# One quarter of the tokens' experts by gathered rows on VectorE, three quarters as dense native fp32 and split products

## The chip, the cores and the metric

The program runs on one core of a Trainium2 chip. Its engines are TensorE (PE, with its weight loads as PEld), VectorE (DVE), ScalarE (ACT), GpSimd (POOL) and SyncE (SP, which here only issues DMAs). The metric is device microseconds of one execution, as a median of several. Everything is float32 at input and output.

## The reference, cut to what matters

The reference runs two two-layer blocks on 256 tokens of width 1024. The first block is not touched. Each layer of the second is a mixing sublayer and then this expert layer, and only the expert layer's arithmetic is arranged anew:

```python
def peer_ffn(xn, wq, sub_keys, u_tab, v_tab):        # xn: 256 tokens x 1024
    q = matmul(xt, wq).reshape(t, 8, 2, 128)          # 8 heads, two half queries
    scores = einsum('thcd,hcnd->thcn', q, sub_keys)   # 128 keys for each half
    sv, si = lax.top_k(scores, 16)
    cand_s = sv[:, :, 0, :, None] + sv[:, :, 1, None, :]
    cand_i = si[:, :, 0, :, None] * 128 + si[:, :, 1, None, :]
    best_s, best_p = lax.top_k(cand_s, 16)            # 16 experts of 16384 a head
    idx = take_along_axis(cand_i, best_p, axis=-1)
    gate = softmax(best_s, axis=-1)
    act = einsum('td,thkd->thk', xb, u_tab[ib])       # 8 x 16 = 128 experts a token
    wgt = gelu(act) * gb
    y = einsum('thk,thkd->td', wgt, v_tab[ib])
```

u_tab and v_tab have 16384 rows of 1024 in each layer. An expert's number is i * 128 + j. A tile of u or v below is [128 x 1024] of 4 bytes, 512 KB: the 128 experts that share a j.

## The kernel before

Each expert layer has three stages, and they run one after the other with a barrier between them.

**choose_stage** streams 16 tiles of query weights (HC = 16) and then the first 28 tiles of u (EARLY = 28) through a ring of four slots (RAW = 4). TensorE works in split precision: ScalarE writes each half tile rounded to fp32r (the high part, line 332), another engine subtracts it from the tile (the low part, line 341; in this stage GpSimd does it), and `product` (line 218) issues three fp32r matmuls, high by high, high by low, low by high. Two split tiles are kept (SPLIT = 2). VectorE meanwhile finds the best keys of each head and then runs a long chain of small operations over candidates, places and gates. TensorE turns three results at the end (line 2320) and uses the last u tile after that.

**scatter_stage** builds, for each token, the 128 x 128 matrix of gates as a native fp32 product of two one-hot matrices (line 2529), in lots of four tokens: 64 lots. VectorE makes the one-hots (line 2498), GpSimd multiplies gates in (line 2517), ScalarE copies the result out (line 2546). Two native fp32 matmuls of 384 columns stand at its end (`hold_clock`, line 2532).

**experts_stage** computes every expert for every token, and the gates, most of them zero, pick. It streams 228 tiles: v tiles 0 to 27, whose activations choose_stage has made, and then u and v in turns for the other 100. A u tile (`activate`) is 24 fp32r matmuls of 256 columns (tokens), on operands h2T (the normalised input, split) and the split tile. ScalarE's gelu (line 2648), then VectorE's multiplication by the gates (2693), rounding (2696) and low part (2698) give the weights of that tile in `chunk`. A v tile (`combine`) is 12 fp32r matmuls of 512 columns: two blocks of 128 tokens by two halves of the width by three passes. Four banks of PSUM hold the sums over all v tiles. ScalarE makes the high part of every tile and VectorE the low part, each in two halves, two tiles ahead of TensorE. SyncE refills a slot as soon as its tile's low part is made. GpSimd has nothing to do in this stage. At its end 16 transposes (line 2635) bring the sums back, and VectorE adds them to x2T (2722).

The order of a u/v pair in the loop is v of j-1, u of j+1, v of j, u of j+2: the weights that a v tile needs come from the u tile two matmul groups earlier.

## Time and profile before

| | us |
|---|---|
| median of 3 runs | 3447.21 |
| lowest and highest | 3446.87, 3452.45 |
| the profiled execution, its own time | 3456.25 |
| its span, first to last instruction | 3454.5 |
| choose, scatter and experts stages of layer 1 | about 76 (after the queries), 87, 642 |

The profile is one execution, read as spans of instructions per engine. "Busy" is the time in which an engine had an instruction under way; idle time is put down to what released the engine after it. TensorE's matmuls overlap, so the time of a group of them is read from the first start to the last end in the timeline, and not as a count times the mean of one.

### The profile page before, as it was taken

The numbers are of one execution on the slowest core, as the hardware profiler recorded it, in microseconds if no ns is written. First come the engines' busy times: TensorE is split into PE (matmuls) and PEld (weight loads), VectorE is DVE, ScalarE is ACT, GpSimd is POOL, SyncE is SP. The second block draws the span as 40 slices with busy tenths as digits, with TensorE's granted clock in tenths as the row PEclk, the third lists the DMA queues.
The fourth block names the chain that finished last, engine by engine and source line by source line (L and its number), as shares of the span: only waits on it lengthen the run. The fifth ranks groups of instructions, "written<-read, shape, count | busy, mean of one in ns | idle before, by whom it ended". The sixth has DMA issues, their size and how long they took to land. (4 is left out here: it accounts for less than half of the span.)

```text
span 3454.5 us, 64762 instructions
## 1 busy us (share of the span) xinstructions
PE 3314.5 (96%) x20448; PEld 2879.7 (83%) x20448; DVE 2427.3 (70%) x4837; ACT 1759.6 (51%) x3349; POOL 543.1 (16%) x444
## 2 busy tenths in 40 slices
PE   7999999999999999999899999999999899999999
PEld 6767777778769998889878989988889878989988
DVE  5567777767566775659877677676659877777676
ACT  4453343333356654656754444444656764454454
POOL 0000000000000000658820000000648830000000
PEclk7999999999899998999999999999999999999999
DMA  5125444435115454335135555555335235555554
GB/s 204 44 69 182 159 138 135 147 122 164 55 61 173 159 174 155 122 117 171 54 128 187 185 187 188 184 187 179 123 116 171 67 115 186 185 188 187 185 187 152
DMA packets 139224, 508.83 MB, mean 147 GB/s; under 512 B 15968, under 2 KB 16352, under 8 KB 138208
## 3 DMA queue, kind: packets, MB, share of 16 engines
q1 hardware_dynamic: 138384, 504.56, 45.0%
q10 hardware_dynamic: 720, 2.71, 0.2%
q8 instruction: 71, 1.16, 0.1%
q14 instruction: 49, 0.40, 0.0%
HBM read 506.16 MB, written 1.05 MB: 147 GB/s over the span
## 5 line engine op out<-in xcount | busy, mean ns | idle before, releaser
L332 ACT ACTIVATE split<-ring 128x512 fp32r<-128x512 f32 (+1 forms) x1660 | 1038.3, 629 | 1390.2 <-PE ps L218 1343.5
L341 DVE TENSOR_TENSOR split<-ring,split 128x512 fp32r<-128x512 f32 (+1 forms) x1364 | 932.0, 687 | 642.9 <-ACT split L332 628.2
L218 PEld LDWEIGHTS ps<-h2T,split 128*128 128x128 f32 x7776 | 946.8, 188 | 30.8 <-DVE h2T L579 5.4
L218 PE MATMUL ps<-h2T,split 128*128 128x256 f32 x7776 | 962.0, 281 | 4.7 <-DVE gates L2135 3.1
L218 PE MATMUL ps<-split,chunk 128*128 128x512 f32 x3072 | 750.4, 395 | 0.0
L341 POOL TENSOR_TENSOR split<-ring,split 128x512 fp32r<-128x512 f32 x296 | 389.6, 1334 | 2174.0 <-ACT split L332 2167.8
L218 PEld LDWEIGHTS ps<-split,chunk 128*128 128x128 f32 x3072 | 561.5, 187 | 124.6 <-DVE chunk L2678 1.1
L218 PE MATMUL ps<-hT,split 128*128 128x512 f32 (+1 forms) x3504 | 631.6, 341 | 6.3 <-DVEq L316 3.4
L218 PEld LDWEIGHTS ps<-hT,split 128*128 128x128 f32 x3504 | 545.1, 190 | 92.6 <-DVE hT L581 7.6
L218 PE MATMUL ps<-act_chunk,split 128*128 128x512 f32 (+1 forms) x1056 | 190.8, 342 | 0.0
L218 PEld LDWEIGHTS ps<-act_chunk,split 128*128 128x128 f32 x1056 | 164.8, 191 | 22.3
L2529 PE MATMUL ps<-ring 128*128 128x128 f32 x1024 | 144.6, 290 | 31.4 <-POOL ring L2517 12.3
L2529 PEld LDWEIGHTS ps<-ring 128*128 128x128 f32 x1024 | 127.7, 197 | 48.2 <-DVE ring L2498 42.4
L2517 POOL TENSOR_TENSOR ring<-ring,slot_gate 128x512 f32<-128x512 f32 x128 | 133.0, 1039 | 32.3 <-DVE ring L2498 32.2
L2693 DVE TENSOR_TENSOR gated<-gelu,gates 128x256 f32<-128x256 f32 x200 | 123.3, 617 | 0.0
L2498 DVE TENSOR_TENSOR ring<-ps,slot_i 128x512 f32<-128x512 f32 x128 | 87.5, 684 | 11.8 <-PEq L2521 11.5
L2698 DVE TENSOR_TENSOR chunk<-gated,chunk 128x256 fp32r<-128x256 f32 x200 | 85.1, 425 | 6.8
L2546 ACT ACTIVATE gates<-ps 128x400 f32 (+1 forms) x128 | 64.4, 503 | 25.8 <-PE ps L2529 24.3
L2648 ACT ACTIVATE gelu<-ps 128x256 f32<-128x256 f32 x200 | 72.8, 364 | 0.0
L2498 DVE TENSOR_TENSOR ring<-ps,slot_j 128x384 f32<-128x384 f32 x128 | 69.8, 545 | 0.0
L218 PE MATMUL ps<-branchT,split 128*128 128x512 f32 (+1 forms) x384 | 69.5, 336 | 0.0
L218 PE MATMUL ps<-y_chunk,split 128*128 128x512 f32 (+1 forms) x384 | 69.5, 340 | 0.0
(353 smaller groups left out, 3166.7 us busy)
## 6 DMA issues: line engine op xcount, KB each, us to landing
ring<-peer_uv SPq DMA_DIRECT2D x456, 512.0 KB, 3.5
ring<-w_up SPq DMA_DIRECT2D x88, 512.0 KB, 3.7
ring<-w_choose SPq DMA_DIRECT2D x88, 512.0 KB, 4.1
ring<-w_mixing SPq DMA_DIRECT2D x68, 512.0 KB, 3.6
ring<-w_merge SPq DMA_DIRECT2D x64, 512.0 KB, 4.1
ring<-w_down SPq DMA_DIRECT2D x44, 512.0 KB, 3.7
mix_row_ring<-w_mod SPq DMA_DIRECT2D x40, 512.0 KB, 3.7
ffn_row_ring<-w_mod SPq DMA_DIRECT2D x40, 512.0 KB, 3.9
```

What stands on the lines that cost most here:

```text
L218: ins = nc.tensor.matmul(out, lhsT(a), rhs(b), start=first and n == 0, stop=last and n == len(PASSES) - 1)
L332: self.nc.scalar.activation(self.split[:, self.half_slot(s), 0, cols], self.ring[:, self.slot(s), cols], ACT.Copy).then_inc(self.high_read ...
L341: (ops or self.nc.vector).tensor_tensor(self.split[:, self.half_slot(s), 1, cols], self.ring[:, self.slot(s), cols], self.split[:, self.ha ...
L2498: nc.vector.tensor_tensor(hot[:, n * lot + first:(n + 1) * lot, :], iota[:, 0:many, :], keys, ALU.is_equal).then_inc(one_hot, 1)
L2517: nc.gpsimd.tensor_tensor(hot, hot, gates, ALU.mult).then_inc(gated, 1)
L2529: last = nc.tensor.matmul(k.ps[:, n, u * NK:(u + 1) * NK], k.hot_i[:, n * lot + u, :], k.hot_j[:, n * lot + u, :], start=True, stop=True)
L2546: nc.scalar.activation(k.dense[:, bass.ds(token(i, n) * late, lot * late)].rearrange("p (t j) -> p t j", t=lot), k.ps[:, n, :].rearrange(" ...
L2648: nc.scalar.activation(k.gelu[:, buf, :], k.ps[:, buf, 0:SEQ], ACT.Gelu_apprx_tanh).then_inc(gelu_done, 1)
L2693: nc.vector.tensor_tensor(k.gated[:, :], k.gelu[:, buf, :], dense[:, :, bass.ds(j - EARLY, 1)].rearrange("p t j -> p (t j)"), ALU.mult).th ...
L2698: nc.vector.tensor_tensor(low, k.gated[:, :], high.bitcast(F32), ALU.subtract).then_inc(weighted, 1)
```

## The change

Tokens 0 to 191 (DENSE = 192) stay in the dense scheme. The 128 experts of each of the last 64 tokens are fetched as rows. Partition p of the row buffers stands for token 192 + p mod 64 and for one half of its 128 experts, so that 64 gathers of u rows and 64 of v rows, each 128 rows of 4 KB (512 KB), serve a layer.

- GpSimd issues the 128 gathers of a layer in experts_stage, by indices `row_at` that VectorE makes in choose_stage, into six slots; each waits until the row six before has been used.
- VectorE takes a dot product of each u row with its token (`dot`, 1024 elements, a multiplication with a running sum), and after one gelu and one multiplication by gates adds each v row times its weight (`add_row`). Their places among the 228 tiles are fixed by a table: one at every v tile from 28 on, one in four before, and 22 more; the first 64 are dots and the last 64 are additions (the table has one place more than it needs).
- u tiles, the early ones in choose_stage and the 100 in experts_stage, are 8 native fp32 matmuls of 192 columns on the raw tile and an unsplit copy of the input (h2F). No high or low part is made of them, and their slot is free only when TensorE has used it.
- A v tile is 10 fp32r matmuls of 512 columns: tokens 0 to 127 keep three passes a half; tokens 128 to 191 stand with their high and low parts side by side in one operand of 128, which meets v's high and low part, two passes a half.
- scatter_stage handles 192 tokens, 48 lots. choose_stage spreads the 64 tokens' inputs over partitions by 16 native fp32 matmuls (`spread_rows`). At the end of experts_stage the sums are turned by one transpose and two native fp32 products with `pair` (64 columns) for each 128 of the width.
- ScalarE's and VectorE's programs in experts_stage are unrolled over the tiles, SyncE's too.
- Buffers move: the gates' buffer gives its last quarter to the row buffers; hT is placed first.

```diff
+DENSE = 192
+ROWS_OF = SEQ - DENSE
+PEER = NK * NK
+ROW_SLOTS = 6
+    def contract_native(self, pe, i, s, out, rhs):
+        pe.wait_ge(self.loaded[s], i * 16 + 16)
+        for c in range(DC):
+            last = self.nc.tensor.matmul(out, self.ring[:, self.slot(s), c * P:(c + 1) * P], rhs(c), start=c == 0, stop=c == DC - 1)
+        last.then_inc(self.halves_used, 2)
@@ choose_stage: SyncE, GpSimd @@
-            weights.load(sp, ahead, count=SPLIT)
+            def slot_free(before):
+                if before < HC:
+                    sp.wait_ge(low_ready, (before + 1) * 2 + int(before == 0))
+                else:
+                    sp.wait_ge(halves_used, weights.used(before // RAW, before % RAW))
+            weights.begin(sp)
+            for t in range(RAW, n_tiles):
+                slot_free(t - RAW)
+                weights.fetch(sp, t // RAW, t % RAW)
+            for s in range(SPLIT):
+                slot_free(n_tiles - RAW + s)
+                ahead.fetch(sp, 0, s)
+            ahead.begun = SPLIT
         @block.gpsimd
         def _(pool):
-            turns(pool, n_tiles, lambda i, s: weights.low(pool, i, s, nc.gpsimd), skip=SPLIT)
+            turns(pool, HC, lambda i, s: weights.low(pool, i, s, nc.gpsimd), skip=SPLIT)
@@ choose_stage: TensorE @@
+            def use_early(i, s):
+                pe.wait_ge(kept, i * RAW + s + 1)
+                weights.contract_native(pe, i, s, k.ps[:, s, 0:DENSE], lambda c: k.h2F[:, c, 0:DENSE])
+            def spread_rows(half):
+                if half == 0:
+                    pe.wait_ge(scores_used, HC + RAW)
+                else:
+                    pe.wait_ge(rows_kept, 1)
+                for c in range(half * HALF, (half + 1) * HALF):
+                    for to in (slice(0, ROWS_OF), slice(ROWS_OF, P)):
+                        last = nc.tensor.matmul(k.ps[to, 2 * RAW - 1, c % HALF * P:(c % HALF + 1) * P],
+                                                k.h2F[:, c, DENSE:SEQ], k.const("ident"), start=True, stop=True)
+                last.then_inc(rows_spread, 1)
...
+                use_early(last_turn, s)
+                if s < 2:
+                    spread_rows(s)
@@ choose_stage: ScalarE @@
+                if s < 2:
+                    act.wait_ge(rows_spread, s + 1)
+                    nc.scalar.activation(k.x_rows[:, s * 512:(s + 1) * 512], k.ps[:, 2 * RAW - 1, :], ACT.Copy).then_inc(rows_kept, 1)
@@ choose_stage: VectorE @@
+            dve.wait_ge(rows_kept, 2)
             nc.vector.tensor_copy(k.ps[:, 2 * RAW - 1, 0:NK], k.const("iota")).then_inc(gate_step, 1)
+            own, at, rows = slice(SLOTS, 2 * SLOTS), k.late_at[:, 0:SLOTS], slice(DENSE - P, P)
+            s(nc.vector.scalar_tensor_tensor(at, k.key_i[:, own], float(NK), k.key_j[:, own], ALU.mult, ALU.add))
+            dve.wait_ge(gate_step, 6)
+            for half in range(2):
+                to, cols = slice(half * ROWS_OF, (half + 1) * ROWS_OF), slice(half * ROWS_OF, (half + 1) * ROWS_OF)
+                for which in range(2):
+                    nc.vector.tensor_scalar(k.row_at[to, which, :], at[rows, cols], float((2 * l + which) * PEER), None, ALU.add).then_inc(step, 1)
+                nc.vector.tensor_copy(k.row_gate[to, :], k.gates[rows, SLOTS + half * ROWS_OF:SLOTS + (half + 1) * ROWS_OF]).then_inc(step, 1)
@@ scatter_stage @@
-    turns_all = SEQ // (lots * lot)
+    turns_all = DENSE // (lots * lot)
@@ experts_stage @@
+    sums = ROWS_OF
+    places = sorted([*range(3, EARLY, 4), *(t for t in range(EARLY, n_tiles) if is_v(t)), *range(EARLY + 1, n_tiles - 8, 9)])
+    dots_at, adds_at = places[:sums], places[-sums:]
+    gelu_at, weigh_at = dots_at[-1] + 1, dots_at[-1] + 2
@@ experts_stage: SyncE, GpSimd @@
-            weights.load(sp, ahead)
+            def slot_free(before):
+                if is_v(before):
+                    sp.wait_ge(low_ready, (v_of(before) + 1) * 2)
+                else:
+                    sp.wait_ge(halves_used, weights.used(before // RAW, before % RAW))
+            weights.begin(sp)
+            for t in range(RAW, n_tiles):
+                slot_free(t - RAW)
+                weights.fetch(sp, t // RAW, t % RAW)
+            if ahead:
+                for s in range(RAW):
+                    slot_free(n_tiles - RAW + s)
+                    ahead.fetch(sp, 0, s)
+                ahead.begun = RAW
             if not norm:
                 for m in range(pairs):
                     sp.wait_ge(added, m + 1)
                     sp.dma_start(out_dram[:, 2 * m:2 * m + 2, :], k.x2T[:, 2 * m:2 * m + 2, :]).then_inc(stored, 16)
                 sp.wait_ge(stored, 16 * pairs)
+        @block.gpsimd
+        def _(pool):
+            for n in range(2 * sums):
+                if n >= ROW_SLOTS:
+                    pool.wait_ge(row_step, n - ROW_SLOTS + 1)
+                at = k.row_at[:, n // sums, n % sums:n % sums + 1]
+                nc.gpsimd.indirect_dma_start(row_slot(n), None, k.peer_rows, bass.IndirectOffsetOnAxis(ap=at, axis=0)).then_inc(
+                    k.rows_in[n % ROW_SLOTS], 16)
@@ experts_stage: TensorE @@
-                weights.contract(pe, i, s, lambda n: k.ps[:, buf, 0:SEQ], lambda c: lambda p: k.hT[:, p, c, :])
+                weights.contract_native(pe, i, s, k.ps[:, buf, 0:DENSE], lambda c: k.h2F[:, c, 0:DENSE])
             def combine(i, s, j, buf, first, last):
                 pe.wait_ge(weighted, j + 3)
                 for half in range(2):
-                    weights.ready(pe, i, s, half)
-                    for b in range(TB):
-                        ins = product(nc, outs[2 * b + half], lambda p: k.weight[:, buf, p, b * P:(b + 1) * P],
-                                      weights.part(s, half * 512, 512), first, last)
+                    pe.wait_ge(low_ready, j * 2 + half + 1)
+                    v = weights.part(buf, half * 512, 512)
+                    product(nc, outs[half], lambda p: k.weight[:, buf, 2 * p * P:(2 * p + 1) * P], v, first, last)
+                    for p in range(2):
+                        ins = nc.tensor.matmul(outs[2 + half], k.weight[:, buf, P:2 * P], v(p), start=first and p == 0, stop=last and p == 1)
                     ins.then_inc(halves_used, 1)
...
+            pe.wait_ge(row_step, 2 * sums)
             for m in range(pairs):
                 pe.wait_ge(kept_0, m // 2 + 1)
                 pe.wait_ge(kept_1, m // 2 + 1)
                 for c in (2 * m, 2 * m + 1):
-                    for b in range(TB):
-                        ins = nc.tensor.transpose(k.ps[:, turned_in[m], c % 2 * SEQ + b * P:c % 2 * SEQ + (b + 1) * P],
-                                                  k.y_natural[:, b, c * P:(c + 1) * P], k.const("ident"))
+                    out, cols = k.ps[:, turned_in[m], c % 2 * SEQ:(c % 2 + 1) * SEQ], slice(c * P, (c + 1) * P)
+                    nc.tensor.transpose(out[:, tokens], k.y_natural[:, 0, cols], k.const("ident"))
+                    nc.tensor.matmul(out[:, both], k.y_natural[:, 1, cols], k.pair[:, :], start=True, stop=True)
+                    ins = nc.tensor.matmul(out[:, DENSE:SEQ], k.y_rows[:, cols], k.pair[:, :], start=True, stop=True)
                 ins.then_inc(turned, 1)
@@ experts_stage: ScalarE @@
+                if is_v(t) and v_of(t) + SPLIT < NK:
+                    high(v_of(t) + SPLIT)
+                if t >= EARLY:
+                    is_u, j, buf = late_tile(t)
+                    if is_u:
+                        activate(t // RAW, t % RAW, j, buf)
+                if t == gelu_at:
+                    act.wait_ge(row_step, sums)
+                    nc.scalar.activation(k.row_act[:, :], k.row_act[:, :], ACT.Gelu_apprx_tanh).then_inc(row_gelu, 1)
@@ experts_stage: VectorE @@
+            def lows(w, buf):
+                for cols, to in ((both, slice(DENSE, 2 * P)), (tokens, slice(2 * P, 3 * P))):
+                    ins = nc.vector.tensor_tensor(k.weight[:, buf, to], w[:, cols], k.weight[:, buf, cols].bitcast(F32), ALU.subtract)
+                ins.then_inc(weighted, 1)
...
-                nc.vector.tensor_tensor(k.gated[:, :], k.gelu[:, buf, :], dense[:, :, bass.ds(j - EARLY, 1)].rearrange("p t j -> p (t j)"),
-                                        ALU.mult).then_inc(weight_step, 1)
+                nc.vector.tensor_tensor(k.gated[:, 0:DENSE], k.gelu[:, buf, 0:DENSE], dense[:, :, j - EARLY], ALU.mult).then_inc(weight_step, 1)
                 dve.wait_ge(weight_step, j * 2 - EARLY + 1)
-                nc.vector.tensor_copy(high, k.gated[:, :]).then_inc(weight_step, 1)
+                nc.vector.tensor_copy(high, k.gated[:, 0:DENSE]).then_inc(weight_step, 1)
                 dve.wait_ge(weight_step, j * 2 - EARLY + 2)
-                nc.vector.tensor_tensor(low, k.gated[:, :], high.bitcast(F32), ALU.subtract).then_inc(weighted, 1)
+                lows(k.gated, buf)
...
+            def dot(n):
+                dve.wait_ge(k.rows_in[n % ROW_SLOTS], rows_there(n))
+                nc.vector.tensor_tensor_reduce(row_slot(n), row_slot(n), k.x_rows, 1.0, 0.0, ALU.mult, ALU.add,
+                                               k.row_act[:, n:n + 1]).then_inc(row_step, 1)
+            def add_row(n):
+                w = k.row_weight[:, n - sums:n - sums + 1]
+                dve.wait_ge(k.rows_in[n % ROW_SLOTS], rows_there(n))
+                if n == sums:
+                    dve.wait_ge(row_weighed, 1)
+                    nc.vector.tensor_scalar(k.y_rows, row_slot(n), w, None, ALU.mult).then_inc(row_step, 1)
+                else:
+                    dve.wait_ge(row_step, n)
+                    nc.vector.scalar_tensor_tensor(k.y_rows, row_slot(n), w, k.y_rows, ALU.mult, ALU.add).then_inc(row_step, 1)
...
+            for t in range(n_tiles):
+                if is_v(t) and v_of(t) + SPLIT < NK:
+                    low(v_of(t) + SPLIT)
+                if t + SPLIT < EARLY:
+                    split_early(t + SPLIT)
+                if t >= EARLY:
+                    is_u, j, buf = late_tile(t)
+                    if is_u:
+                        weigh(t, j, buf)
+                for n in [n for n, at in enumerate(dots_at) if at == t]:
+                    dot(n)
+                if t == weigh_at:
+                    dve.wait_ge(row_gelu, 1)
+                    nc.vector.tensor_tensor(k.row_weight[:, :], k.row_act[:, :], k.row_gate[:, :], ALU.mult).then_inc(row_weighed, 1)
+                for n in [n for n, at in enumerate(adds_at) if at == t]:
+                    add_row(sums + n)
@@ second_block @@
+    tail = Carver(gates[:, DENSE * NK:])
+    k.early = gates[:, 0:EARLY * DENSE].rearrange("p (j t) -> p j t", j=EARLY)
+    k.dense = gates[:, EARLY * DENSE:DENSE * NK]
+    k.x_rows, k.y_rows, k.row_ring = tail(D), tail(D), tail(ROW_SLOTS, D)
```

Late in the first layer's experts stage, in the loop over u and v tiles, TensorE's row of one turn's second half reads so before (a u tile, then a v tile; chunk holds the weights, h2T the input):

```order
L376 ISA
L218 MATMUL ps<-h2T,split 128x256 x12
L376 REGISTER_ALU
L218 MATMUL ps<-h2T,split 128x256 x12
L2608 REGISTER_ALU
L376 ISA
L218 MATMUL ps<-split,chunk 128x512 x6
L376 REGISTER_ALU
L218 MATMUL ps<-split,chunk 128x512 x6
```

and so in the changed kernel:

```order
L2694 REGISTER_ALU
L399 ISA
L401 MATMUL ps<-h2F,ring 128x192 x8
L2701 REGISTER_ALU
L2703 ISA
L224 MATMUL ps<-split,chunk 128x512 x3
L2707 MATMUL ps<-split,chunk 128x512 x2
L2703 REGISTER_ALU
L224 MATMUL ps<-split,chunk 128x512 x3
L2707 MATMUL ps<-split,chunk 128x512 x2
```

The u tile's 24 matmuls became 8 that read the ring itself, and the v tile's 12 became 10.

VectorE, in the first turn of the u and v tiles, before: low parts (341) of both kinds of tile, then gates, rounding and low part of the weights (2693, 2696, 2698).

```order
L341 TENSOR_TENSOR split<-ring,split 128x512 x2
L2693 TENSOR_TENSOR gated<-gelu,gates 128x256
L2696 CAST chunk<-gated 128x256
L2698 TENSOR_TENSOR chunk<-gated,chunk 128x256
L341 TENSOR_TENSOR split<-ring,split 128x512 x4
L2693 TENSOR_TENSOR gated<-gelu,gates 128x256
L2696 CAST chunk<-gated 128x256
L2698 TENSOR_TENSOR chunk<-gated,chunk 128x256
```

In the changed kernel a pair of tiles reads as follows. Line 2819 is the v tile's low part, 2826 a dot (its second row hands over the sum), 2808, 2810 and 2788 the weights.

```order
L2819 TENSOR_TENSOR split<-ring,split 128x512 x2
L2826 ISA gates,row_act<-gates 128x1024
L2826 ISA row_act 128x1
L2808 TENSOR_TENSOR gated<-gelu,gates 128x192
L2810 CAST chunk<-gated 128x192
L2788 TENSOR_TENSOR chunk<-gated,chunk 128x64
L2788 TENSOR_TENSOR chunk<-gated,chunk 128x128
```

Of four low parts per pair two are left, and a dot (or an addition, later) stands between the low parts and the weights.

## Rows read from the trace of the kernel before

**Rows 1.** The page: busy time of each engine and its share of the span.
```profile
PE 3314.5 (96%) x20448; PEld 2879.7 (83%) x20448; DVE 2427.3 (70%) x4837; ACT 1759.6 (51%) x3349; POOL 543.1 (16%) x444
```

**Rows 2.** Busy time by stretch, layer 1: choose after queries, scatter, early v, pairs.
```profile
core 0: us, PE busy (x) PEld busy (x) DVE busy (x) ACT busy (x) POOL busy (x), PEclk, DMA share, GB/s
1593.20:1669.80 76.60, 76.60 (x665) 76.41 (x663) 70.96 (x176) 57.37 (x95) 70.27 (x54) 1.00 0.56 173
1673.90:1760.70 86.80, 73.85 (x518) 65.15 (x518) 82.14 (x195) 68.79 (x192) 66.53 (x64) 0.96 0.00 0
1760.70:1839.20 78.50, 78.50 (x337) 63.33 (x337) 54.72 (x110) 34.65 (x55) 0.00 (x0) 1.00 0.61 201
1839.20:2402.10 562.90, 562.90 (x3600) 507.07 (x3600) 396.00 (x700) 279.17 (x499) 0.00 (x0) 1.00 0.57 186
```

**Rows 3.** Timeline of one u/v pair: start and length in us; TensorE.
```profile
2005.47 2.99 PE L218 MATMUL ps<-h2T,split 128*128 128x256 f32 x24
...
2008.29 2.96 PE L218 MATMUL ps<-split,chunk 128*128 128x512 f32 x12
```

**Rows 4.** Timeline at the routing logits, TensorE: ten native fp32 records of 256 columns.
```profile
1497.64 2.32 PE L1814 MATMUL ps<-gates 128*128 128x256 f32 x10
```

**Rows 5.** The same line's instructions: ns, shortest, median and longest.
```profile
L1814 PE MATMUL ps<-gates x32: 377/378/484, 1497.6 to 2556.5; 128*128 128x256 f32 x32
```

**Rows 6.** Groups by line and shape, whole span: xcount, busy us, mean ns.
```profile
L2529 PE MATMUL ps<-ring 128*128 128x128 f32 x1024 | 144.6, 290 | 31.4 <-POOL ring L2517 12.3 <-DVE ring L2498 9.6 <-issue 7.7
L218 PE MATMUL ps<-h2T,split 128*128 128x256 f32 x7776 | 962.0, 281 | 4.7 <-DVE gates L2135 3.1 <-DVE h2T L579 0.8 <-DVE gates L2051 0.7
L218 PE MATMUL ps<-split,chunk 128*128 128x512 f32 x3072 | 750.4, 395 | 0.0
L332 ACT ACTIVATE split<-ring 128x512 fp32r<-128x512 f32 x1636 | 1027.0, 631 | 1349.4 <-PE ps L218 1302.7 <-PE ps L1832 22.8 <-DMA ring<-peer_uv 10.7
L341 DVE TENSOR_TENSOR split<-ring,split 128x512 fp32r<-128x512 f32 x1340 | 920.5, 690 | 621.8 <-ACT split L332 607.1
L2693 DVE TENSOR_TENSOR gated<-gelu,gates 128x256 f32<-128x256 f32 x200 | 123.3, 617 | 0.0
L2696 DVE CAST chunk<-gated 128x256 fp32r<-128x256 f32 x200 | 58.7, 294 | 6.9
L2698 DVE TENSOR_TENSOR chunk<-gated,chunk 128x256 fp32r<-128x256 f32 x200 | 85.1, 425 | 6.8
L448 DVE SCALAR_TENSOR_TENSOR const_sb<-ffn_row_ring,cond_silu,const_sb 128x1024 f32<-128x1024 f32 x42 | 52.0, 1278 | 0.0
```

**Rows 7.** Waits within 1842 to 2400 us: total us, times, longest us.
```profile
ACT split L332 <- PE ps L218: 279.4, 395, 0.8
DVE split L341 <- ACT split L332: 152.6, 250, 0.8
```

**Rows 8.** DMA issues, KB each and median us to landing: 1842 to 2400 us.
```profile
ring<-peer_uv SPq DMA_DIRECT2D x194, 512.0 KB, 3.5
```

**Rows 9.** The same for 9 to 66 us.
```profile
ring<-w_mod SPq DMA_DIRECT2D x12, 512.0 KB, 5.0
```

**Rows 10.** Busy time by stretch (columns as in rows 2), DMA at its fullest.
```profile
429.00:439.00 10.00, 10.00 (x45) 8.20 (x44) 8.88 (x11) 3.36 (x6) 0.00 (x0) 1.00 1.02 410
```

**Rows 11.** Timeline of TensorE: transposes at the ends of choose and experts.
```profile
1666.22 0.82 PE L2320 MATMUL ps<-const_sb,gates 128*128 128x128 f32 x6
1666.79 3.08 PE L218 MATMUL ps<-h2T,split 128*128 128x256 f32 x24
...
2403.41 1.94 PE L2635 MATMUL ps<-const_sb,gates 128*128 128x128 f32 x16 [0.87 <-DVE gates L2718]
```

**Rows 12.** Timeline of VectorE beside GpSimd, choose stage of layer 1.
```profile
1618.98 0.28 DVE L2427 TENSOR_SCALAR gates<-gates 128x256 uint32<-128x256 uint32 x1
1619.10 29.68 POOL L341 TENSOR_TENSOR split<-ring,split 128x512 fp32r<-128x512 f32 x22 [0.19 <-ACT split L332]
1619.18 1.38 DVE L2428 TENSOR_SCALAR gates<-gates 128x256 uint32<-128x256 uint32 x1
...
1628.72 1.67 DVE L2435 TENSOR_TENSOR gates<-gates 128x512 f32<-128x512 f32 x1
```

163 lines of the change are left out of this document (83 added, 80 removed).

## The prediction

> **What bounds the kernel now.** I read the page first: of 3454.5 us TensorE is busy for 96%, no other engine for more than 70% [rows 1]. Busy PE is not PE at its peak, so I then read the stages of the second block, whose expert layers are all that the change touches [rows 2]. The reader is to see that in the experts stage TensorE is busy for every microsecond of its 78.5 + 562.9 us, at full clock (1.00, the 2.4 GHz level), with VectorE at 396.0 of 562.9, ScalarE at half and the DMA engines at a share of 0.57. The waits there say the same: ScalarE waits 279.4 us for TensorE to free split buffers, VectorE 152.6 us for ScalarE, and nobody keeps TensorE [rows 7]. In the scatter stage it is otherwise: VectorE has 82.1 of 86.8 us, TensorE waits. After the queries choose_stage is again TensorE's, 76.6 of 76.6 us. Time is therefore saved in two stages by shortening TensorE's row, in one by doing fewer lots, as long as nothing else takes its place.
>
> The change is summed for layer 1 and doubled; layer 2 has the same stages.
>
> **What a matmul costs.** Of n matmuls in a row the distance is (length minus one duration) / (n - 1). A u tile's 24 take 2.99 us with one of 0.281, so 0.118 each and 2.83 a tile; a v tile's 12 take 2.96 with one of 0.395, so 0.233 each and 2.80 [rows 3, 6]. A pair is 562.9 / 100 = 5.63 us.
>
> **The u tile.** Eight native products look like a third of the work. The trace says that they are not: line 2529 is one matmul for each of 512 tokens, and has 1024 records [rows 6], that is two. A native fp32 matmul is two passes in the trace. Each pass takes, at 256 columns, (2.32 - 0.378) / 9 = 0.216 us [rows 4, 5], and an fp32 record of 128 columns (1.94 - 0.290) / 15 = 0.110 [rows 6, 11], 0.85 ns a column. At 192 columns that is between them, 0.163, or 0.161 by the column, and a tile is 16 x 0.161 = 2.58; I take 2.60. It saves 0.23 us of 2.83, by the quarter of the columns that are gone and not by fewer instructions. Bounds: 16 x 0.155 = 2.48, and 16 x 0.216 = 3.46 if a pass of 192 cost as much as one of 256 (nothing in the rows suggests it; 0.161 is between two measured points).
>
> **The v tile.** 10 matmuls of 512 columns instead of 12: 10 x 0.233 = 2.33, saving 0.47. TensorE's row for a pair becomes 2.60 + 2.33 = 4.93.
>
> **What comes up behind TensorE.** Four costs have to fit beneath 4.93 us a pair.
>
> VectorE: two low parts 2 x 0.690; weights of 192 columns: the gates' product 0.617 at 256 becomes about 0.50, the rounding 0.294 becomes 0.26, and the low part of 0.425 becomes two of 64 and 128 columns. Between 0.425 at 256 and 0.690 at 512 a column costs 1.04 ns, so these are 0.23 and 0.29 [rows 6]. Together 2.66. A dot or an addition over 1024 elements with two operands in SBUF is like line 448, 1.28 us [rows 6], and a dot also hands over its sum, for which I add 0.1. In the pairs there are 121 row steps to 100 pairs: 1.21 x 1.33 = 1.61. Sum 4.3 us: 87% of 4.93. Not the bound, but close.
>
> DMA: two tiles and 1.21 rows, 3.21 x 0.524 MB = 1.68 MB. At its fullest the trace has 410 GB/s at a share of 1.02 [rows 10], so 4.1 us, a share of 0.83 where it was 0.57.
>
> ScalarE: it has 279 of 562.9 us busy [rows 2] and loses half of its high parts. No matter.
>
> The chain of one v tile's load: this is what I expect to end last. Before, a slot was free as soon as its tile was split. Now a u tile's slot is free only when TensorE has used it, and SyncE's queue is in order, so the v tile behind it waits too. From the end of u tile j+1, SyncE fetches a u tile and then v tile j+2; L later that has landed, ScalarE makes two high parts (1.26), VectorE the second low part (0.69), then a row step (1.28 to 1.38), then the weights of j+2 (1.28), and with a few hand-overs TensorE may start v tile j+2. That is L + 4.6. TensorE is there after exactly two pairs, so a pair takes the larger of 4.93 and (L + 4.6) / 2. A lone tile lands in 3.5 us [rows 8]; a second one right behind it adds its transfer, 0.524 MB / 410 GB/s = 1.28: L = 4.8, nothing lost. With a gathered row between them it is 6.1 and a pair takes 5.35. When the engines are nearly full in the trace the median landing is 5.0 [rows 9]. I take L of 5.4 in the mean, hence 5.0, and 0.05 for the pairs with two row steps in the chain: **5.05 us a pair**, 505 us, which is 57.9 less than 562.9.
>
> **Early v tiles.** 28 at 2.33 on TensorE; VectorE has 1.38 + 0.78 + a quarter of 1.38 = 2.5 less overlaps. I take 2.40: 67.2 for 78.5, 11.3 less.
>
> **Scatter.** 64 lots take 86.8 us with about 4 of start and end: 1.28 a lot [rows 2]. 48 lots: 20.4 us less.
>
> **Choose.** 28 u tiles in 76.6 us less 0.6 for transposes [rows 11] are 2.71 each. At 2.60 they save 3.1. But `spread_rows` puts 16 native matmuls, 32 passes of 128 columns at about 0.11, before the last of them: 3.5 us. VectorE's chain no longer has GpSimd's splitting beside it, and gets some ten microseconds shorter: the same kind of operation takes 0.28 us before GpSimd starts and 1.38 beside it [rows 12]. That gains nothing, as TensorE ends the stage. The indices for the gathers (seven small operations of VectorE, and their waits) lie beside TensorE's transposes and last tile. Net +0.4.
>
> **Ends.** Six gathers are issued at the stage's start, 3.1 MB beside the first v tiles: +1.5. At the end each 128 of the width has four more short native passes, 8 x 4 x 0.11 = 3.5, less two transposes' worth and what lies beside VectorE's additions: +1.5. First block, mixing: 0; hT's new place could change nothing or a per cent of a matmul's distance, and no row tells which.
>
> **Sum.** -57.9 - 11.3 - 20.4 + 0.4 + 3.0 = -86.2 a layer, -172 for both. Against the profiled span 3454.5 that is 3282; the profiled execution's own time (3456.25) lies 9 above the median of 3447.21, so against the median: 3447 - 172 = **3275 us**.
>
> **Rivals.**
> *VectorE becomes the bound.* GpSimd is idle in this stage now and will issue 128 gathers. Beside a working GpSimd, operations of VectorE with two inputs in SBUF take 1.67 instead of 0.69 [rows 6, 12]. If a gather holds VectorE for g us, VectorE's pair is 4.3 + 1.21 g. At g = 1 that is 5.5, or with rows landing late as much: 3275 + 2 x 100 x 0.45 = 3365. For it: rows 12. Against: GpSimd there runs elementwise work over 512 columns without a pause; here it writes addresses for 128 rows.
>
> *Slower than before, by the same place.* The savings outside the pairs and the 0.58 in them are used up when a pair takes 5.05 + 0.86 = 5.91, so with g above 1.33 us, or when GpSimd needs over 5.91 / 1.21 = 4.9 us to issue one gather. At g = 1.8 a pair takes 6.5: 3275 + 200 x 1.45 = 3565. Nothing in the trace issues a gather; so g is bounded by 0 and by GpSimd's own longest operation, 29.68 / 22 = 1.35 us each at line 341 [rows 12], or several of those.
> The Trainium skill (SBUF — State Buffer, "Who interferes with whom") says that a VectorE instruction with two SBUF inputs contends with a GpSimd instruction that reads SBUF, not with one that only writes it, and infers that descriptor generation needs the write side. By it g is near 0, dots and additions go on beside the gathers, and only the 0.26 us rounding could be held up. By rows 12 alone g could be 1. I lean to the page, and no run before shows it.
>
> *The native product is cheaper than I think,* or two records are not two passes. Then a u tile is 1.3 us, TensorE's pair 3.6, and VectorE at 4.3, or the load chain at 4.6 to 5.0, sets the pair: 3275 - 200 x 0.45 = 3185.
>
> *The clock falls.* In the scatter stage TensorE waits for VectorE in each lot and keeps 0.96 to 1.00 [rows 2]; at 4.93 of 5.05 it is busier than that. Not likely.
>
> **How the numbers follow.** Forecast, a pair of 4.86 to 5.3 us (3237 to 3325): 0.56. VectorE or late loads, 5.3 to 5.85 (3325 to 3435): 0.22. Slower (above 3454, mostly 3480 to 3620): 0.13. Cheaper native products (3150 to 3235): 0.07. Close to no change: 0.02. The range takes in the forecast and most of the second: 3225 to 3400. A measurement of this kernel tells 0.2% (7 us) from no change. Faster by more: 0.85, within: 0.02, slower: 0.13.
>
> **What the profile after would show.** In the pairs: matmuls of 192 columns 16 a tile, 0.16 apart; the pair at 5.0 to 5.1; small gaps of TensorE before a v tile that end with VectorE's low part of the weights (2788), or before a tile with a DMA. A dot at 1.3 us; if it is 2 or more beside gathers, it is the second rival. The DMA share near 0.8. Scatter at 66 us. VectorE's chain in choose without its 1.4 us operations, and no gain from it. I would be wrong if a dot took over 2 us, if a gather landed later than six row steps (30 us), or if TensorE idled more than half a microsecond a pair.

## The result and the profile after

The changed kernel takes 3431.75 us (median of 9 runs, 3411.18 to 3438.51) against 3452.45 us of the kernel before (9 runs, 3444.83 to 3457.53). The ratio is 0.9942, 95% interval 0.9926 to 0.9957: faster by 0.6%, where 5% were forecast and the range ended at 3400. The profiled execution spans 3424.7 us.

The page's busy times (engine, us, share of the span, instructions), beside [rows 1]:

```profile
PE 3161.7 (92%) x17744; PEld 2709.8 (79%) x17744; DVE 2348.6 (69%) x4997; ACT 1367.4 (40%) x2735; POOL 635.9 (19%) x556
```

TensorE lost 153 us of work and the span lost 30. The table by stretch says where the rest went. The stretches are choose after the queries, scatter, early v tiles and pairs of layer 1, then the pairs of layer 2; the columns are those of [rows 2].

```profile
1598.80:1674.70 75.90, 75.90 (x489) 75.07 (x487) 61.43 (x197) 21.75 (x40) 2.02 (x2) 1.00 0.55 180
1681.10:1742.40 61.30, 55.39 (x384) 48.35 (x385) 58.70 (x140) 51.43 (x139) 48.78 (x47) 0.96 0.00 0
1745.30:1816.80 71.50, 67.78 (x281) 51.21 (x281) 57.11 (x145) 32.56 (x52) 12.93 (x12) 1.00 0.86 305
1816.80:2387.50 570.70, 512.67 (x2600) 451.44 (x2599) 383.50 (x781) 140.94 (x303) 123.16 (x116) 0.99 0.82 291
2839.30:3415.30 576.00, 512.85 (x2601) 452.38 (x2599) 383.74 (x781) 139.24 (x301) 123.11 (x116) 0.99 0.80 284
```

Measured in both kernels from a stage's first matmul to its last:

| stage (us) | forecast per layer | layer 1 | layer 2 |
|---|---|---|---|
| choose | +0.4 | 78.2 to 75.9 | 78.2 to 75.9 |
| scatter | -20.4 | 81.8 to 61.3 | 81.3 to 61.6 |
| early v tiles | -11.3 | 78.5 to 71.5 | 78.5 to 71.5 |
| 100 pairs | -57.9 | 562.9 to 570.7 | 562.9 to 576.0 |

So the small stages came out nearly as forecast, and the pairs, which were to bring two thirds of the gain, got longer: 5.71 and 5.76 us each instead of 5.05. TensorE now has 512.7 us of work in 570.7, neither VectorE (383.5) nor the DMA engines (0.82) are full. It is a chain of waits, and the waits of the pairs in layer 1 name it (who waited for what: us in total, times, longest us):

```profile
ACT split L2754 <- DMA ring<-peer_uv: 398.0, 98, 7.7
DVE split L2819 <- ACT split L2754: 179.3, 78, 5.7
PE ps L224 <- DVE chunk L2788: 57.9, 46, 5.2
```

Before, ScalarE waited for TensorE [rows 7]. Now ScalarE waits for a landing ahead of every high part, VectorE for ScalarE, and TensorE for weights that VectorE makes. One turn of it in the timeline (start and length in us; what is in brackets is the idle time ahead and its releaser):

```profile
2003.26 10.66 SPq L255 DMA_DIRECT2D ring<-peer_uv  x6
...
2007.99 1.15 ACT L2754 ACTIVATE split<-ring 128x512 fp32r<-128x512 f32 x2 [4.39 <-DMA ring<-peer_uv]
...
2008.65 1.29 DVE L2819 TENSOR_TENSOR split<-ring,split 128x512 fp32r<-128x512 f32 x2 [3.73 <-ACT split L2754]
...
2009.05 0.31 ACT L2746 ACTIVATE gelu<-ps 128x192 f32<-128x192 f32 x1
...
2009.86 1.22 DVE L2826 CUSTOM_DVE_ANT_0 gates<-gates 128x1024 f32<-128x1024 f32 x1
...
2011.01 0.08 DVE L2826 DVE_READ_ACCUMULATOR2_ANT row_act<- 128x1 f32 x1
2011.01 1.22 DVE L2826 CUSTOM_DVE_ANT_0 gates<-gates 128x1024 f32<-128x1024 f32 x1
...
2012.15 0.51 DVE L2808 TENSOR_TENSOR gated<-gelu,gates 128x192 f32<-128x192 f32 x1
2012.70 0.42 DVE L2810 CAST chunk<-gated 128x192 fp32r<-128x192 f32 x1
...
2013.15 0.43 DVE L2788 TENSOR_TENSOR chunk<-gated,chunk 128x64 fp32r<-128x64 f32 x2
...
2013.72 0.96 PE L224 MATMUL ps<-split,chunk 128*128 128x512 f32 x3 [0.64 <-DVE chunk L2788]
```

The v tile that TensorE starts at 2013.72 has had its own low part since 2009.94 and waits for its weights alone, made from 2012.15 to 2013.58. Their gelu was done at 2009.36. They stood in VectorE's queue behind that low part and behind two dots; and the low part stood behind the landing of the same v tile, the second fetch of SyncE's row (issued at 2003.6).

### The profile page after: what moved, and what is told of

Its sections match the earlier page's. It is cut to its first block and busy times, and to the rows that moved or that the text cites. A ratio compares the mean times of both kernels' runs of the same rounds, so it can differ in the third digit from the quotient of the medians.

```text
span 3424.7 us, 52815 instructions
## 1 busy us (share of the span) xinstructions
PE 3161.7 (92%) x17744; PEld 2709.8 (79%) x17744; DVE 2348.6 (69%) x4997; ACT 1367.4 (40%) x2735; POOL 635.9 (19%) x556
## 3 DMA queue, kind: packets, MB, share of 16 engines
q10 hardware_dynamic: 720, 2.71, 0.2%
## 5 line engine op out<-in xcount | busy, mean ns | idle before, releaser
L401 PE MATMUL ps<-h2F,ring 128*128 128x192 f32 x4096 | 702.3, 327 | 0.0
L401 PEld LDWEIGHTS ps<-h2F,ring 128*128 128x128 f32 x4096 | 679.5, 191 | 19.3 <-issue 0.7
L338 ACT ACTIVATE split<-ring 128x512 fp32r<-128x512 f32 (+1 forms) x644 | 398.2, 624 | 703.1 <-PE ps L224 665.0
L2754 ACT ACTIVATE split<-ring 128x512 fp32r<-128x512 f32 x504 | 296.3, 625 | 897.6 <-DMA ring<-peer_uv 829.4
L2819 DVE TENSOR_TENSOR split<-ring,split 128x512 fp32r<-128x512 f32 x504 | 328.2, 688 | 388.0 <-ACT split L2754 385.9
L347 DVE TENSOR_TENSOR split<-ring,split 128x512 fp32r<-128x512 f32 (+1 forms) x460 | 308.2, 679 | 291.0 <-ACT split L338 289.5
L2687 POOL DMA_INDIRECT gates<-peer_rows,row_at x256 | 272.3, 1064 | 993.9 <-DVE row_act L2826 545.8
L224 PE MATMUL ps<-h2T,split 128*128 128x256 f32 x1632 | 209.1, 285 | 4.8 <-DVE gates L2147 4.0
L224 PEld LDWEIGHTS ps<-h2T,split 128*128 128x128 f32 x1632 | 198.9, 191 | 12.4 <-DVE h2T L591 5.4
L2837 DVE SCALAR_TENSOR_TENSOR gates<-gates,row_weight 128x1024 f32<-128x1024 f32 x126 | 161.2, 1280 | 1.5
L2826 DVE CUSTOM_DVE_ANT_0 gates<-gates 128x1024 f32<-128x1024 f32 x128 | 155.3, 1219 | 0.0
```

Of the source, the lines that this page charges most:

```text
L224: ins = nc.tensor.matmul(out, lhsT(a), rhs(b), start=first and n == 0, stop=last and n == len(PASSES) - 1)
L338: self.nc.scalar.activation(self.split[:, self.half_slot(s), 0, cols], self.ring[:, self.slot(s), cols], ACT.Copy).then_inc(self.high_read ...
L347: (ops or self.nc.vector).tensor_tensor(self.split[:, self.half_slot(s), 1, cols], self.ring[:, self.slot(s), cols], self.split[:, self.ha ...
L401: last = self.nc.tensor.matmul(out, self.ring[:, self.slot(s), c * P:(c + 1) * P], rhs(c), start=c == 0, stop=c == DC - 1)
L2687: nc.gpsimd.indirect_dma_start(row_slot(n), None, k.peer_rows, bass.IndirectOffsetOnAxis(ap=at, axis=0)).then_inc(k.rows_in[n % ROW_SLOTS] ...
L2754: nc.scalar.activation(weights.split[:, weights.half_slot(j), 0, cols], weights.ring[:, weights.slot(t), cols], ACT.Copy).then_inc(high_re ...
```

## The experiments

Three explanations stood against each other. **A**: the in-order chain fetch, high part, low part, row step, weights, TensorE, from the end of one u tile to the v tile that TensorE reaches two pairs later. **B**: VectorE is too full, or held up by the gathers. **C**: with gathered and plain transfers mixed, the DMA engines give no more than the 291 GB/s of the pairs. Pairs are given for layer 1, from the first matmul of the first u tile to the last v tile.

### The split one place later

```diff
             for t in range(n_tiles):                     # ScalarE
-                if is_v(t) and v_of(t) + SPLIT < NK:
-                    high(v_of(t) + SPLIT)
+                if t < EARLY:
+                    high(t + SPLIT)
...
                         activate(t // RAW, t % RAW, j, buf)
+                        if t > EARLY + 2:
+                            high(j)
...
-                if is_v(t) and v_of(t) + SPLIT < NK:     # VectorE
-                    low(v_of(t) + SPLIT)
+                if t < EARLY:
+                    low(t + SPLIT)
...
                     add_row(sums + n)
+                if t > EARLY + 2 and not is_v(t):
+                    low(late_tile(t)[1])
```

> The same work, only each v tile's high part (ScalarE) and low part (VectorE) come one place later in their engines' programs: behind the gelu, the weights and the row step of the u tile between, so that no weights wait behind a split whose tile has not landed. Theory A (the in-order chain load, high, low, row step, weights, TensorE, which now lasts 6.6 + 4.8 us for two pairs, sets 5.72 us a pair): the weights leave the chain, it falls to 6.6 + 2.0 for two pairs, TensorE's own 4.9 us decides, pairs at 4.9 to 5.0, time 3432 - 200 x 0.77 = 3278 us. Theory B (VectorE bound or held up by the gathers): the same work on VectorE, so 5.7 a pair and about 3430. Theory C (the DMA engines give no more than the 298 GB/s seen with both queues): same bytes, 5.7 a pair and about 3430.

Measured: 3299.31 us, ratio to the kernel before 0.9569 (0.9539 to 0.9598). The pairs take 509.5 us, 5.10 each. Theory A holds; B and C expected no change. It is 21 us over A's figure: TensorE now waits a little for the low part itself, and 5.3 us once at the start of the pairs.

```profile
1804.20:2313.70 509.50, 499.53 (x2601) 447.99 (x2599) 387.08 (x781) 147.84 (x303) 125.42 (x116) 0.99 0.91 325
```

That is the row of the pairs by stretch, and this one of their waits:

```profile
PEld ps L224 <- DVE split L2821: 7.2, 14, 1.2
```

### Only SyncE's order of fetches

```diff
-            for t in range(RAW, n_tiles):
+            order = list(range(RAW, n_tiles))
+            for t in range(EARLY + RAW - 1, n_tiles - 1, 2):
+                if not is_v(t) and is_v(t + 1):
+                    order[t - RAW], order[t + 1 - RAW] = t + 1, t
+            for t in order:
                 slot_free(t - RAW)
                 weights.fetch(sp, t // RAW, t % RAW)
```

> The same work, only SyncE's queue in the pairs fetches each v tile ahead of the u tile that it stood behind, so that the v tile's fetch waits for its own slot's low part alone. Theory A: the v tile then lands about 2.5 us or more earlier against TensorE, the chain of 11.4 us for two pairs is closed at the low part and not at the end of the u tile, pairs at 4.9 to 5.1, time about 3285 us. Theories B and C: same work and same bytes, 5.7 a pair, about 3430.

Measured: 3285.11 us, ratio 0.9528 (0.9498 to 0.9558), the figure that A gave. No engine does another instruction, and no byte is added or left out: 68 us of the 570.7 went by exchanging neighbours in one queue.

```profile
1808.80:2311.10 502.30, 495.22 (x2600) 448.30 (x2599) 387.59 (x781) 152.04 (x303) 125.81 (x116) 0.99 0.92 331
```

C falls with it: the same bytes now move at 331 GB/s. So does the first form of B: VectorE's busy time is the same (387.6 for 383.5) in a stretch 68 us shorter.

### Row steps of 16 elements

```diff
-nc.vector.tensor_tensor_reduce(row_slot(n), row_slot(n), k.x_rows, 1.0, ...
+nc.vector.tensor_tensor_reduce(row_slot(n)[:, 0:16], row_slot(n)[:, 0:16], k.x_rows[:, 0:16], 1.0, ...
```

and the additions alike.

> Every dot and every addition of VectorE works on 16 of the 1024 elements (the last 64 tokens' sums are left out but for that); all 128 gathers of a layer stay. Theory A: each row step of 1.2 to 1.3 us in the chain becomes about 0.1, two pairs take 11.4 - 1.4 = 10.0, so 5.0 a pair and 3290 us. Theory B: VectorE has 2.9 us a pair, TensorE decides, 4.9 and 3270. Theory C (bytes): unchanged, 5.7 a pair and 3430.

Measured: 3365.62 us (one run), 5.42 a pair. The direction is A's, C is excluded again, but only 0.29 of A's 0.72 us a pair came, so A's account was too simple. The table under "The load chain" below has the parts of the chain for this kernel too. In the mean it got 0.87 us shorter and not 1.4: the row steps take 1.15 less of it, the fetches 0.35 more (6.00 for 5.65 us). And the chain comes round once in three pairs and not in two, as is worked out there: 0.87 / 3 = 0.29.

```profile
1822.60:2364.30 541.70, 508.94 (x2600) 449.02 (x2599) 258.67 (x783) 139.09 (x303) 112.66 (x116) 0.99 0.86 306
```

### Only six gathers a layer

```diff
-            for n in range(2 * sums):
+            for n in range(ROW_SLOTS):
...
-    rows_there = lambda n: 16 * (l * len(...) + n // ROW_SLOTS + 1)
+    rows_there = lambda n: 16 * (l + 1)
```

> Only the first six gathers of a layer are made, and the row steps use those six again and again (the other rows' share of the result is left out; the product of a dot goes to another buffer of the same size). VectorE's work is unchanged. Theory A: two fetches issued together land in 3.5 + 1.3 instead of 5.9 us, the chain is 5.4 + 4.8 for two pairs, 5.1 a pair, 3305 us. Theory B in the form that VectorE's own work is too long: unchanged, 3430; in the form that gathers hold VectorE up: its dots and low parts get shorter, which the trace would show. Theory C: 1.05 MB a pair, TensorE decides, 4.9 and 3270.

Measured: 3311.54 us (one run), 5.11 a pair, A's figures. VectorE's dots are as long as before (1.218 us in the mean, 1.219 with gathers), so the gathers cost nothing on VectorE. What they cost lies in the fetches. By the trace's packet records a v tile's fetch lasts 4.03 us in the mean from issue to last packet here and 5.65 with the gathers; the transfers of a row get in between those of the tiles. In the changed kernel the 17 of 94 fetches with fewer than 60 gather packets begun before their own last one took 4.3 us in the mean, the 47 with 130 or more 6.2.

```profile
1819.80:2330.90 511.10, 497.47 (x2601) 448.20 (x2599) 381.05 (x779) 138.53 (x301) 0.00 (x0) 1.00 0.57 205
```

### Both of these

> The changed kernel's orders, with row steps over 16 elements and only six gathers a layer (the last 64 tokens' sums are left out). The chain of two pairs has fetches of 4.0 us, as in e1_six_gathers, and about 1.1 less of VectorE's: some 8.5 us, under TensorE's 9.8. Theory A: TensorE alone decides, pairs at 4.9, and 5.3 us of waiting once a layer at the start of the pairs: about 3270 us. If a third cause beside gathers and row steps kept the pairs at 5.7, it would show here as pairs over 5.0.

Measured: 3271.59 us (one run); the pairs take 499.1 us of which TensorE has 495.0. The chain is down to 8.2 us here, under the 9.55 from which on TensorE waits, and no third cause keeps the pairs apart.

### Longer row steps, in either order

```diff
                 dve.wait_ge(k.rows_in[n % ROW_SLOTS], rows_there(n))
+                nc.vector.tensor_tensor(row_slot(n), row_slot(n), k.x_rows, ALU.mult).then_inc(row_extra, 1)
+                dve.wait_ge(row_extra, n + 1)
                 nc.vector.tensor_tensor_reduce(...)
```

> The changed kernel with one more multiplication over 1024 elements of VectorE in front of every dot and every addition, 1.28 us and a semaphore of 0.06 each (the rows' values are changed by it). Theory A (the chain load, high, low, row step, weights of two pairs): the chain of 11.4 to 11.6 us gets 1.34 us longer, 0.7 a pair, VectorE has 5.9 of 6.4 us: 3432 + 140 + 15 in the first v tiles = about 3585 us. Theory B (VectorE bound, the extra work adds in full): 1.62 a pair, about 3770 us. Theory C (bytes): VectorE's 5.9 becomes the larger, 3432 + 40 = 3475 us.

> e5_fetch_swap with the extra multiplication of e3_long_rows (1.34 us a row step). VectorE has 4.34 + 1.21 x 1.34 = 5.96 us a pair, now more than TensorE's 4.9. If with the fetch order mended VectorE's plain sum is the bound: pairs at 6.0, 14 us more in the first v tiles of each layer: 3285 + 200 x 0.95 + 28 = about 3500 us, 65 below e3_long_rows. If the chain through the loads still ran: 3566, as e3_long_rows.

Measured (one run each): 3565.90 us in the changed kernel's order (6.28 a pair), 3390.51 with the fetches exchanged (5.44 a pair). The same work, 175 us apart. In the first VectorE is busy for 524.7 of 628.3 us (and the granted clock is 0.95 there, so a part of the 6.28 is TensorE's); in the second for 97% of a stretch within the pairs, so there VectorE is the bound at last. My 3500 for it was too high by a way of counting: I had 5.96 us a pair of single durations. They add up to 5.67 in the trace, as the extra operation takes 1.22 and not 1.34, and neighbours on VectorE overlap by 0.08 each, so its busy time is 5.2 a pair. A's figure for the first, 3585 us, fits within 20, and the second lies well below it, as A says; B's 3770 does not fit. The row of the pairs of the first kernel:

```profile
1822.20:2450.50 628.30, 534.27 (x2601) 467.49 (x2599) 524.70 (x901) 142.37 (x301) 122.50 (x116) 0.95 0.75 264
```

and of the stretch from 1832 to 2360 us in the second:

```profile
1832.00:2360.00 528.00, 490.89 (x2547) 438.75 (x2545) 512.26 (x884) 152.00 (x299) 120.41 (x114) 1.00 0.87 308
```

### The start of the pairs

With the fetches exchanged one long wait of TensorE was left in each layer:

```profile
1815.12 1.15 ACT L2758 ACTIVATE split<-ring 128x512 fp32r<-128x512 f32 x2 [3.62 <-DMA ring<-peer_uv]
1815.78 1.29 DVE L2823 TENSOR_TENSOR split<-ring,split 128x512 fp32r<-128x512 f32 x2 [3.47 <-ACT split L2758]
1816.17 0.53 ACT L2750 ACTIVATE gelu<-ps 128x192 f32<-128x192 f32 x2
...
1819.43 1.65 PE L224 MATMUL ps<-split,chunk 128*128 128x512 f32 x3 [5.32 <-DVE chunk L2792]
```

The gelus of u tiles 28 and 29 stand on ScalarE behind the split of v tile 29, whose fetch waits for u tile 28 to be used. The edit (VectorE's alike, and the exchange of fetches begins two tiles later):

```diff
-                if is_v(t) and v_of(t) + SPLIT < NK:
+                if is_v(t) and v_of(t) + SPLIT < NK and t != EARLY - 1:
                     high(v_of(t) + SPLIT)
...
                         activate(t // RAW, t % RAW, j, buf)
+                if t == EARLY + 1:
+                    high(EARLY + 1)
```

> As e5_fetch_swap (each v tile of the pairs fetched ahead of its u tile), and the split of v tile 29 comes behind the gelus and weights of u tiles 28 and 29 instead of ahead of them. In e5_fetch_swap TensorE has one wait of 5.3 us in each layer, ahead of v tile 28: ScalarE and VectorE stand at the split of v tile 29, whose fetch waits for u tile 28 to be used, and the weights of v tile 28 are behind it. Expected: that wait goes, and the two slower v tiles behind it (about 2 us), 7 us a layer: 3285 - 14 = 3271 us. If the wait has another cause: 3285.

Measured: 3264.64 us (3252.06 to 3267.24), ratio to the kernel before 0.9467 (0.9451 to 0.9483). This is the best of the kernels here. Of the 31 us between its profiled execution and that of the exchange alone, 16 lie in the pairs of the two layers; 10 lie ahead of the expert layers, in code that the edit does not touch. TensorE has no time left in the pairs:

```profile
1799.30:2294.10 494.80, 493.77 (x2600) 447.13 (x2599) 385.53 (x781) 150.86 (x303) 126.90 (x116) 1.00 0.92 335
```

### No row steps among the early v tiles

```diff
-    places = sorted([*range(3, EARLY, 4), *(t for ... if is_v(t)), *range(EARLY + 1, n_tiles - 8, 9)])
+    places = sorted([*(t for ... if is_v(t)), *range(EARLY + 1, n_tiles - 1, 7)])
```

> As e7_swap_start, and no row step lies among the first 28 v tiles; they lie among the 200 tiles of the pairs, every seventh tile instead of every ninth getting one more. If VectorE's queue sets the first 28 v tiles (it has 1.38 + 0.75 a tile there and 1.3 more in every fourth), they fall from 71.4 to about 66.5 us, TensorE's own 2.33 to 2.4 a tile, and the pairs, where TensorE decides, stay at 5.0: 3271 - 10 = 3261 us. If the six first gathers' transfers set them: unchanged, 3271.

Measured: 3276.98 us, ratio 0.9514 (0.9484 to 0.9545): no gain on the run before it, where 10 us were expected. In its profile the early v tiles do fall from 71.2 to 67.8 us, so VectorE's queue did set them; the pairs rise from 494.8 to 497.3. The profiled executions are 21 us apart, and 19 of these lie ahead of the expert layers, in code that neither edit touches (the last query matmul comes at 1600.5 instead of 1581.6 us); the first block's own changes are taken up below.

### Both remedies

> Both remedies together: v tiles fetched ahead of their u tiles from tile 33 on, and every split of the pairs behind the gelu, the weights and the row step of the u tile between. In e7_swap_start TensorE has 4.92 us of the 4.94 of a pair, so if TensorE is what is left the time stays at 3265 us, within 7. If the 4.94 still hides waits for weights behind splits, up to 4 us less. If the row steps ahead of the low part now make TensorE wait for it (as 0.09 us a v tile in e4_late_split), 5 to 10 us more.

Measured: 3299.50 us, ratio 0.9562 (0.9539 to 0.9585). Together they take 35 us more than the exchange with the mended start alone, and no case of the expectation has that; the pairs have 511.0 us for 494.8, and as much in layer 2. As I read the edit, a low part made later frees the v tile's slot later; its fetch goes out later; and the u tile's fetch now stands behind it. TensorE's waits in the pairs are indeed for u tiles now:

```profile
PEld ps L401 <- DMA ring<-peer_uv: 12.5, 20, 1.2
PEld ps L401 <- issue: 12.5, 20, 1.8
PE ps L401 <- DMA ring<-peer_uv: 9.4, 17, 1.4
```

### The price of a native product

```diff
-                weights.contract_native(pe, i, s, k.ps[:, buf, 0:DENSE], lambda c: k.h2F[:, c, 0:DENSE])
+                for c in range(DC):
+                    for p in range(3):
+                        ins = nc.tensor.matmul(k.ps[:, buf, 0:DENSE], k.hT[:, p // 2, c, 0:P], k.hT[:, p % 2, c, 0:DENSE], ...)
```

> As e5_fetch_swap, but each of the 100 u tiles of the pairs is 24 fp32r matmuls of 192 columns on constant operands of that type instead of 8 native fp32 products on the ring (the u tile's values are left out). It prices the native product against the split one at this width, with no splitting work on ScalarE and VectorE. If an fp32r matmul costs by the column as at 256 columns (0.118 us), 24 x 0.0885 = 2.12 us a tile against 2.46: pairs at 4.7, 3285 - 65 = 3220 us. If 192 columns cost what 256 do: 2.83 a tile, pairs at 5.4, 3285 + 75 = 3360 us.

Measured: 3300.28 us (one run), 5.10 a pair, between the two cases. TensorE's timeline in this kernel:

```profile
2000.68 2.82 PE L2702 MATMUL ps<-h2T 128*128 128x192 f32 x24
2003.34 0.87 PE L224 MATMUL ps<-split,chunk 128*128 128x512 f32 x3
```

and in the changed one:

```profile
2000.47 2.76 PE L401 MATMUL ps<-h2F,ring 128*128 128x192 f32 x16
2002.94 0.99 PE L224 MATMUL ps<-split,chunk 128*128 128x512 f32 x3
```

24 fp32r matmuls of 192 columns are 0.111 us apart, (2.82 - 0.27) / 23, hardly less than the 0.118 at 256 columns [rows 3]; 16 native passes are 0.162 apart, (2.76 - 0.33) / 15. With the v tile behind it a turn of TensorE is 5.01 us against 4.93 (the next u tile starts at 2005.69 and at 2005.40). So the native product is worth 0.1 us a pair on TensorE, and otherwise what it saves ScalarE and VectorE in splits. Most of TensorE's gain is the quarter of the tokens that left.

## Why the prediction was wrong, step by step

**TensorE's work: right.** A native pass of 192 columns was put at 0.161 us and takes 0.162. A pair of TensorE was put at 4.93 and is 4.92 wherever nothing waits. That a native product is two passes held too: a u tile has 16 records and takes 2.61 us.

**VectorE: right as a sum, not as a load.** 4.3 was forecast, the durations add up to 4.24. But busy time is 383.5 us for 100 pairs, 3.8 each, since neighbours overlap by 0.08 us (487 times, 39.8 us in all). It had more room than I gave it.

**The second rival, gathers that hold VectorE up: did not come.** g is 0. The dots' shortest, median and longest are 1216, 1219 and 1222 ns; only the rounding and a gather's own issue lengthen each other now and then (23 roundings of 200, each beside a gather's issue; 163 more lay beside one and kept their 0.26 us):

```profile
L2826 DVE CUSTOM_DVE_ANT_0 gates<-gates x128: 1216/1219/1222, 1757.6 to 3118.6; 128x1024 f32<-128x1024 f32 x128
L2810 DVE CAST chunk<-gated x200: 259/260/452, 1826.6 to 3412.3; 128x192 fp32r<-128x192 f32 x100
L2687 POOL DMA_INDIRECT gates<-peer_rows,row_at x256: 938/972/1933, 1745.2 to 3397.4; - x128
```

With six gathers a layer the rounding's longest is 263 ns, so the 452 belong to the gathers. The Trainium skill (SBUF — State Buffer, "Who interferes with whom") says just this: two-input operations are left alone by a GpSimd instruction that only writes SBUF, and copies and casts in a two-port mode can be held up. The trace agrees on both. Dots and additions beside gathers never took longer, as the operations of [rows 12] did beside GpSimd's splitting.

**The load chain: the right path, and the term that failed.** The chain that I expected to end last (theory A) is the one that did. I wrote: a pair takes the larger of 4.93 and (L + 4.6) / 2, with L = 5.4, hence 5.0. So I put the chain at 10.0 us, and it is 11.2; that sum is the step that failed. The trace's records give the parts for 94 v tiles of layer 1, in us (the issue from SyncE's record, the last packet from the packets' records):

| part, mean us | forecast | changed kernel | short rows | six gathers |
|---|---|---|---|---|
| u tile's end to v tile's issue | 0 | 0.41 | 0.42 | 0.41 |
| issue to last packet | | 5.65 | 6.00 | 4.03 |
| last packet to start of high part | | 0.40 | 0.41 | 0.35 |
| the last two together | 5.4 (L) and about 0.1 | 6.05 | 6.41 | 4.38 |
| high part's start to low part's end | 1.95 | 2.07 | 1.97 | 1.96 |
| row step and first operations of weights | 2.1 | 2.09 | 0.94 | 2.06 |
| last weights | 0.5 | 0.43 | 0.43 | 0.43 |
| hand-over to TensorE (shortest) | 0 | 0.14 | 0.14 | 0.14 |
| the chain | 10.0 | 11.18 | 10.31 | 9.38 |
| v tiles for which TensorE waited | | 50 of 94 | 44 of 94 | 12 of 94 |

- *L was 0.6 too short.* It runs to the landing, as the 3.5 of [rows 8] does. By the records of the landings' semaphores a v tile landed 6.0 us after its issue in the mean, not 5.4; the last packet comes 0.3 to 0.4 us before that. The prediction's own case "with a gathered row between them" had 6.1, and 5.35 us a pair; I took a mean too near to the case without one.
- *What follows on L was 0.6 too short.* 5.2 instead of 4.6. Of this 0.41 is the way from the u tile's end to the v tile's issue (SyncE issues the u tile's fetch first), which stood at nothing; the rest is hand-overs and turns in which a part waits its turn. 12 of the 94 v tiles have two row steps in the chain, as in the timeline above.
- *The cycle has three pairs, not two.* The chain of v tile j starts at the end of u tile j-1. From the start of v tile j TensorE needs 5.21 us to the end of u tile j+2 (a pair of 4.92, and the 0.29 by which each tile's first matmul starts ahead of the last one's end in the records), where the chain of v tile j+3 starts. So one wait serves three pairs: once a chain C is longer than 9.55 us (2 x 4.92 - 0.29), a pair takes (C + 5.21) / 3. At 10.0 that is 5.07, and that the forecast's rule came near it there was luck. At 11.18 it is 5.46, where the forecast's rule would have said 5.6.
- *The spread.* Single fetches last from 4.0 to 7.8 us, as gathers fall in or not. A short chain gives nothing back, so the mean of the chains understates the pairs. If each v tile starts at the later of the end of its own measured chain and TensorE's own turn, the three kernels come out at 5.62, 5.35 and 5.04 us a pair; measured over the same v tiles are 5.66, 5.37 and 5.04. With six gathers the mean chain, 9.38, is under the 9.55, and the 12 longest still cost 0.12 a pair.

So of the 0.66 us by which layer 1's 5.71 misses 5.05, some 0.4 are the mean chain, 0.2 the spread, and 0.05 a wait of 5.2 us at the start of the pairs. Layer 2, whose chains were not taken apart, misses 5.05 by 0.71. Together these are 137 of the 143 us between the forecast and the result in the profiled executions (3282 and 3424.7).

**Early v tiles:** 71.5 for 67.2 a layer, 9 us in all. VectorE's queue was put at 2.5 a tile "less overlaps", and I took less than it costs: 2.55. Without row steps it is 67.8.

**Choose and ends:** -2.3 a layer for +0.4. The early u tiles save more than I had, since choose_stage took 78.2 us before and not the 76.6 of my stretch, which began 1.6 us late: 2.77 a tile, not 2.71. And the 16 products of `spread_rows` take 2.2 us and not 3.5; their records of 64 by 128 are 0.054 us apart ((1.09 - 0.27) / 15), half of what I took from a full tile:

```profile
1664.01 1.09 PE L2330 MATMUL ps<-const_sb,h2F 128*64 128x128 f32 x16
```

Scatter was right, 20.5 and 19.7 for 20.4. The ends, put at +3.0 a layer, came to +1.4 behind layer 1 and -0.5 behind layer 2.

**The first block** was put at 0. In the profiles it ends 7.4 us later (the last query matmul at 1598.8 for 1591.4), at a granted clock of 0.92 instead of 0.94 in its first 500 us:

```profile
0.00:500.00 500.00, 458.80 (x2048) 350.75 (x2049) 329.24 (x616) 207.80 (x420) 5.21 (x8) 0.92 0.38 133
```

The mean clock of all 9 runs is 0.963 to 0.968. In the 23 runs of the kernel before that stand beside the experiments it is 0.972 to 0.978, with the fetches exchanged 0.966 to 0.970, and with the start mended as well 0.974 to 0.977. The cause is open.

**The rivals and chances.** Slower got 0.13, and "VectorE or late loads, 5.3 to 5.85 us a pair" 0.22; its late loads are what came. The result lies inside that case (3325 to 3435), and outside the range only because I cut it at 3400, in the middle of the case. The prediction's sign of being wrong, TensorE idle for over half a microsecond a pair, came too: (570.7 - 512.7) / 100 = 0.58. The time that was forecast does exist in this kernel: 3264.64 us, with the order of one queue changed and one split moved.

## What to carry to other kernels

When a slot's release moves from an early reader (a split) to a late one (a matmul), look at everything that stands behind it in the in-order queues: the DMA queue's next fetch, the split behind that landing, and the small operation behind that split which the bottleneck needs now. Add up such a chain with every hand-over at its measured length, and compare its spread, not its mean, with the bottleneck's period. Count also how many turns pass until the chain comes round to itself: what a chain is too long is paid once in so many turns, and what it is shortened comes back at the same rate. Exchanging two neighbours in the fetch order was worth 4% here; doing two remedies at once was worth less than one.

## What the hardware showed that was not expected

- An fp32r matmul of 192 columns starts 0.111 us after its neighbour, one of 256 columns 0.118. The 64 columns fewer bring next to nothing, while a native fp32 pass falls by the column (0.162 at 192, 0.216 at 256 [rows 4]).
- 116 gathers of 512 KB within 571 us leave VectorE's dots at their length to 3 ns. A gather keeps GpSimd for 0.97 us (median), and its last packet comes 5.7 us after its issue in the mean, where that of a plain 512 KB fetch without gathers came after 3.1 (the landing after 3.5 [rows 8]).
- Packets of gathers and of tile fetches alternate in the records: a v tile's fetch of 4.0 us became 5.65, at a DMA share of 0.82 instead of 0.57.
